# A state-space mixer's chunk stage on one core: two program blocks joined into one, with decay buffers, carried state, gate and squares placed differently

## The reference

```python
def ssd_chunked(x, dt, a, bmat, cmat):        # 256 tokens, 16 heads of 64, 2 groups, state 128
    l = SSD_CHUNK                              # 128, so c = 2 chunks
    xd = (x * dt[..., None]).reshape(b, c, l, g, r, p)
    a_cs = cumsum((dt * a) within a chunk)
    seg = exp(where(causal, a_cs[l] - a_cs[s], -inf))
    cb = einsum('bclgn,bcsgn->bcgls', cm, bm)
    y_diag = einsum('bcgrls,bcsgrp->bclgrp', cb * seg, xd)
    states = einsum('bclgn,bcgrl,bclgrp->bcgrpn', bm, exp(a_cs[-1] - a_cs), xd)
    y_off = einsum('bclgn,bcgrpn,bcgrl->bclgrp', cm, state carried in, exp(a_cs))
    return y_diag + y_off
...
    y = ssd_chunked(...) + xs * d_skip         # mamba2_branch
    y = y * silu(z)
    yg = y * rsqrt(mean(y * y over the group) + eps)
    return yg * norm_w
```

## Time and profile before

| | us |
|---|---|
| median of 3 runs | 2144.39 (2143.79 to 2147.41) |
| profiled execution | 2136.68 |
| its span, first to last instruction | 2134.7 |
| PE busy in the span | 1880.7 |
| DVE busy | 1016.3 |
| ACT busy | 589.1 |
| mean granted TensorE clock | 0.898 of full |

### The profile page before, as it was taken

How to read it: one execution, slowest core, us unless ns; L and a number is a source line. 1 busy time by engine, 2 the same in 40 slices (tenths; PEclk the granted TensorE clock), 3 DMA queues, 4 the chain that set the end, 5 groups by cost and what they waited for, 6 DMA issues and landing times. The chain is left out here.

```text
span 2134.7 us, 33193 instructions
## 1 busy us (share of the span) xinstructions
PE 1880.7 (88%) x14404; PEld 1474.7 (69%) x14404; DVE 1016.3 (48%) x1903; ACT 589.1 (28%) x865; POOL 25.5 (1%) x16
## 2 busy tenths in 40 slices
PE   4999999789999699989984799979996996758998
PEld 3544356574443599968863699979995875547997
DVE  5122243332222566623474565656666156656664
ACT  3000012320000533312241443344332222024332
POOL 0000000000000100000000010010000000001000
PEclk8789899787998899999976899999998998579999
DMA  6799960359999555414210355535550411034540
GB/s 271 327 424 425 425 255 19 134 207 359 425 424 425 218 184 191 153 60 181 98 58 0 119 181 194 178 128 183 183 183 23 167 55 61 4 138 141 194 158 20
DMA packets 57993, 404.28 MB, mean 189 GB/s; under 512 B 6352, under 2 KB 7760, under 8 KB 10224
## 3 DMA queue, kind: packets, MB, share of 16 engines
q1 hardware_dynamic: 57840, 402.07, 49.5%
HBM read 400.99 MB, written 1.05 MB: 188 GB/s over the span
## 5 line engine op out<-in xcount | busy, mean ns | idle before, releaser
L1717 PE MATMUL ps<-ffn_xh,ffn_wh 128*128 128x256 f32 x1408 | 405.2, 288 | 28.5 <-DVE ffn_xl L1832 28.5
L1718 PE MATMUL ps<-ffn_xl,ffn_wh 128*128 128x256 f32 x1408 | 403.5, 287 | 0.0
L1719 PE MATMUL ps<-ffn_xh,ffn_wl 128*128 128x256 f32 x1408 | 403.1, 286 | 0.0
L1808 DVE TENSOR_TENSOR ffn_wl<-w,ffn_wh 128x2048 fp32r<-128x2048 f32 (+1 forms) x136 | 304.3, 2237 | 15.9 <-ACT ffn_wh L1774 14.7
L1717 PEld LDWEIGHTS ps<-ffn_xh,ffn_wh 128*128 128x128 f32 x1408 | 275.7, 196 | 31.1 <-DVE ffn_wl L1808 29.5
L1718 PEld LDWEIGHTS ps<-ffn_xl,ffn_wh 128*128 128x128 f32 x1408 | 275.7, 196 | 1.6
L1719 PEld LDWEIGHTS ps<-ffn_xh,ffn_wl 128*128 128x128 f32 x1408 | 275.5, 196 | 0.0
L1774 ACT CAST ffn_wh<-w 128x2048 fp32r<-128x2048 f32 (+1 forms) x136 | 247.1, 1842 | 18.4 <-PEq L2229 8.2
L1815 DVE TENSOR_TENSOR ffn_zg<-ps,rs 128x256 f32<-128x256 f32 x88 | 37.4, 425 | 247.8 <-PE ps L1719 247.6
L1788 ACT ACTIVATE ffn_sil<-ffn_zg 128x256 f32<-128x256 f32 x88 | 36.8, 418 | 419.6 <-DVE ffn_zg L1815 419.6
L1717 PE MATMUL ps<-ffn_wh,ffn_hidh 128*128 128x512 f32 x352 | 137.4, 390 | 0.0
(11 more groups left out here) (481 smaller groups left out, 2829.2 us busy)
## 6 DMA issues: line engine op xcount, KB each, us to landing
w<-in_ffn_gu SPq DMA_DIRECT2D x88, 1024.0 KB, 5.0
w<-in_moe_gu SPq DMA_DIRECT2D x78, 1024.0 KB, 16.0
w_extra<-in_moe_gu SPq DMA_DIRECT2D x50, 1024.0 KB, 21.0
w<-in_ffn_dn SPq DMA_DIRECT2D x44, 1024.0 KB, 5.0
w_extra<-in_moe_dn SPq DMA_DIRECT2D x32, 1024.0 KB, 18.0
w<-in_moe_dn SPq DMA_DIRECT2D x32, 1024.0 KB, 21.5
w<-in_ab_xbc SPq DMA_DIRECT2D x6, 1024.0 KB, 4.8
w<-in_ab_out SPq DMA_DIRECT2D x6, 1024.0 KB, 4.9
```

The source lines that it names most:

```text
L1717: nc.tensor.matmul(out, wh, xh, start=start, stop=False)
L1718: nc.tensor.matmul(out, wh, xl, start=False, stop=False)
L1719: return nc.tensor.matmul(out, wl, xh, start=False, stop=stop)
L1808: nc.vector.tensor_tensor(low[:, s, at], S.buf(units[n])[:, at], high[:, s, at], ALU.subtract).then_inc(*w_split.one())
```

## The change

`ssd_chunks` becomes one block. The sum computed is the same; what moves:

- `seg` has three buffers (u % 3). On DVE, weigh(u) stands ahead of relative(u + 1).
- On PE, decays(0) and decays(1) stand among the transposes, and decays(u + 2) stands behind values(u). The state's two products stand behind decays(4), and what the state gives to chunk 1 behind decays(6). The B features and `cb` use banks 7 and 6 at first, the transposes of `xs` banks 2 to 5, which are also those of values.
- ACT begins with the Silu of `z`, then the two small Exps; it copies chunk 1's `xs` from banks 4 and 5 behind exp(0) and exp(1). Its squares write a buffer `junk` instead of `xd`; those of chunk 0 follow exp(7), those of chunk 1 wait for its gate, and each waits for the one before.
- On DVE, one more step stands between relative(u) and weigh(u) or between two units: `xd` of chunk 1, the skip product of either chunk, the copy of the state, and for chunk 0 adding the products and the gate. After the loop the carried part is scaled into a buffer `off` and added in one instruction for both groups, and then chunk 1 has its products added and its gate.

The diff, cut; the removed side is the function printed above:

```diff
-        seg = sb("ssd_seg", [P, 2, 4, P])
+        seg = sb("ssd_seg", [P, 3, 4, P])
...
+            def decays(u):
+                if u >= 2:
+                    pe.wait_ge(*s_ready.at(u - 1))
...
+            def values(u):
+                pe.wait_ge(*ready.at(u + 1))
+                pe.wait_ge(*xd_made.at(c + 1))
...
+            turn_x(0)
+            decays(0)
+            turn_x(1)
...
+            decays(1)
+            turn_x(2)
+            turn_x(3)
...
+            for u in range(n):
+                if u == 4:
+                    pe.wait_ge(*xs_taken.at(2))
+                values(u)
+                if u + 2 < n:
+                    decays(u + 2)
+                if u == 2:
+                    states()
+                if u == 4:
+                    carried()
...
+            nc.scalar.activation(z[:], z[:], ACT.Silu)
+            nc.scalar.activation(acs[:, 0, 1], acs[:, 0, 1], ACT.Exp)
+            nc.scalar.activation(acs[:, 1, 2], acs[:, 1, 0], ACT.Exp).then_inc(*e_done.one())
...
+            for u in range(n):
+                act.wait_ge(*s_ready.at(u + 1))
+                nc.scalar.activation(seg[:, u % 3], seg[:, u % 3], ACT.Exp).then_inc(*e_made.one())
+                if u < 2:
+                    act.wait_ge(*made.at(4 + u))
+                    nc.scalar.copy(xs[:, 1, 512 * u:512 * u + 512], K.ps[:, 4 + u]).then_inc(*xs_taken.one())
+            link(act, K.act_step, squares(0))
+            link(act, K.act_step, squares(1))
...
+            def relative(u):
+                dve.wait_ge(*s_made.at(u + 1))
+                if u >= 3:
+                    dve.wait_ge(*y_made.at(u - 2))
...
+            def gate(c):
+                dve.wait_ge(*y_made.at(4 * c + 4))
...
+            weigh(1)
+            relative(2)
+            dve.wait_ge(*xs_taken.at(2))
+            v.tensor_tensor(hp(xd[:, 1]), hp(xs[:, 1]), heads(dt[:, 1]), ALU.mult).then_inc(*xd_made.one())
+            weigh(2)
+            relative(3)
+            skip(0)
+            weigh(3)
+            relative(4)
+            dve.wait_ge(*st_made.at(1))
+            v.tensor_copy(state[:], K.ps[:, 6:8].rearrange("p g n -> p g n")).then_inc(*st_taken.one())
+            weigh(4)
+            relative(5)
...
+            skip(1)
+            weigh(5)
+            relative(6)
+            gate(0)
+            weigh(6)
+            relative(7)
+            weigh(7)
```

More of the change, by code:

```diff
@@ L2315, in ssd_chunks @@
     hp = lambda ap: ap.rearrange("p (h d) -> p h d", d=HD)
+    wide = lambda ap: ap.rearrange("p (h a) -> p h a", a=1)
+    units = [(c, g, q) for c in range(2) for g in range(SSD_GROUPS) for q in range(2)]
+    n = len(units)
     with ExitStack() as ctx:
@@ L2323, in ssd_chunks @@
         state = sb("ssd_state", [P, SSD_GROUPS, HG * HD])
+        off = sb("ssd_off", [P, SSD_INNER])
+        junk = sb("ssd_junk", [P, 512])
+        seg = sb("ssd_seg", [P, 3, 4, P])
         ms = sb("ssd_ms", [P, 2, SSD_GROUPS, 2])
[L2325 to L2336, removed]
-                mm.then_inc(*made.one())
[L2338 to L2342, removed]
@@ new lines, in ssd_chunks @@
+        made, xs_taken, e_done = K.sig("tile_made"), K.sig("fill_taken"), K.sig("exp_done")
+        st_in, st_made, st_taken, off_made = K.sig("exp_asked"), K.sig("t_made"), K.sig("t_taken"), K.sig("o_taken")
+        s_made, s_ready, e_made, ready, y_made = K.sig("s_made"), K.sig("s_ready"), K.sig("e_made"), K.sig("p_ready"), K.sig("pv_made")
+        xd_made, gated, rooted = K.sig("x_ready"), K.sig("gated"), K.sig("rooted")
+        block = ctx.enter_context(nc.Block())
+        @block.sync
@@ L2346, in _ @@
                 mm.then_inc(*st_made.one())
[L2348 to L2372, removed]
@@ L2374, in ssd_chunks, with carried @@
-        units = [(c, g, q) for c in range(2) for g in range(SSD_GROUPS) for q in range(2)]
-        n = len(units)
-        seg = sb("ssd_seg", [P, 2, 4, P])
[L2377 to L2386, removed]
+            def carried():
+                pe.wait_ge(*st_taken.at(1))
@@ L2387, in _ @@
                 for g in range(SSD_GROUPS):
                     mm = nc.tensor.matmul(K.ps[:, 6 + g], cv[:, 10 + g, P:2 * P], state[:, g], start=True, stop=True)
[L2389 to L2441, removed]
-                dve.wait_ge(*y_made.at(n))
-                dve.wait_ge(*y_off.at(1))
-                for c in range(2):
-                    do(v.tensor_tensor(hp(xs[:, c]), hp(xs[:, c]), wide(row[:, 2]).to_broadcast([P, 16, HD]), ALU.mult))
-                    for g in range(SSD_GROUPS):
-                        part = xs[:, c, g * 512:(g + 1) * 512]
-                        do(v.tensor_tensor(part, part, K.ps[:, 2 + 2 * c + g], ALU.add))
-                        if c == 1:
-                            tmp = xdd[:, g * 512:(g + 1) * 512]
-                            do(v.tensor_tensor(hp(tmp), hp(K.ps[:, 6 + g]), wide(acs[:, 1, 2, g * HG:(g + 1) * HG]).to_broadcast([P, HG, HD]), ALU.mult))
-                            do(v.tensor_tensor(part, part, tmp, ALU.add))
-                last = v.tensor_tensor(xs[:], xs[:], z[:], ALU.mult)
-                last.then_inc(*used.one())
-                dve.wait_ge(*used.at(2))
-                do(v.reciprocal(ms[:, :, :, 0:1], ms[:, :, :, 1:2]))
-                for c in range(2):
-                    for g in range(SSD_GROUPS):
-                        at = g * 512
-                        last = v.scalar_tensor_tensor(out=joined[:, c, 512 + at:1024 + at], in0=xs[:, c, at:at + 512], scalar=ms[:, c, g, 0:1],
-                                               in1=normw[:, at:at + 512], op0=ALU.mult, op1=ALU.mult)
@@ new lines, in carried @@
+                mm.then_inc(*off_made.one())
+            turn_x(0)
+            decays(0)
+            turn_x(1)
+            for c in range(2):
+                for g in range(SSD_GROUPS):
+                    t = slice(c * P, (c + 1) * P)
+                    mm = nc.tensor.matmul(K.ps[:, 6, (2 * c + g) * P:(2 * c + g + 1) * P], cv[:, 8 + g, t], cv[:, 10 + g, t], start=True, stop=True)
+            mm.then_inc(*made.one())
+            decays(1)
+            turn_x(2)
+            turn_x(3)
@@ new lines, in _ @@
+            for g in range(SSD_GROUPS):
+                mm = nc.tensor.transpose(K.ps[:, 7, g * P:(g + 1) * P], cv[:, 8 + g, 0:P], K.con(C_ID))
+            mm.then_inc(*made.one())
+            for u in range(n):
[8 more added lines that the diff above has]
+                    carried()
@@ new lines, in _, with squares @@
+        @block.scalar
+        def _(act):
+            nc.scalar.activation(z[:], z[:], ACT.Silu)
+            nc.scalar.activation(acs[:, 0, 1], acs[:, 0, 1], ACT.Exp)
+            nc.scalar.activation(acs[:, 1, 2], acs[:, 1, 0], ACT.Exp).then_inc(*e_done.one())
+            def squares(c):
+                act.wait_ge(*gated.at(c + 1))
+                for g in range(SSD_GROUPS):
+                    last = nc.scalar.activation(junk[:], xs[:, c, g * 512:(g + 1) * 512], ACT.Square, accum_out=ms[:, c, g, 0:1])
+                    if g < SSD_GROUPS - 1:
+                        link(act, K.act_step, last)
+                return last
+            for u in range(n):
[6 more added lines that the diff above has]
+            link(act, K.act_step, squares(1))
+            nc.scalar.activation(ms[:, :, :, 1:2], ms[:, :, :, 0:1], ACT.Sqrt, bias=K.eps[:, 1:2], scale=1.0 / (HG * HD)).then_inc(*rooted.one())
```

71 lines of the change are left out of this document (added).

## The result

| | before | after |
|---|---|---|
| median | 2144.09 us (2141.49 to 2147.41, 4 runs) | 2108.82 us (2107.87 to 2113.50, 4 runs) |
| traced execution | 2136.68 | 2108.55 |
| its span | 2134.7 | 2106.8 |
| the stage in it | 68.06 | 40.85 |
| ahead of the stage | 1110.50 | 1109.62 |

The recorded ratio is 0.9844 (95% interval 0.9828 to 0.986), which is 33 us of gain (30 to 37); the two medians lie 35.3 us apart. The stage of the trace did almost what was worked out: 27.2 us less for 26.9. So the question is where the other 6 to 8 us are: the two traces differ by 27.9 us in span, the medians by 35.3.

What follows compares the result with a forecast made beforehand. The prediction took engines waiting for each other as the bound. Start 3.87, DVE's work 30.87 and tail 6.40 us replaced the 68.06 us stage: 26.9 us less, 2144.39 to 2117.5 us, range 2112 to 2125.

Steps and rivals of the forecast that it cites:

- What bounds the stage, and where its waits are: Changed stage: engines wait for each other; DVE waited 19.5 us for PE's decays, ACT 26.3 us for DVE's relative.
- Part 1: Loop: DVE's 2.82 us covers PE's 2.14, so DVE stops waiting except 0.79 us at weigh(7); third buffer costs nothing.
- Part 2: Stage start: DVE's second copy of chunk 0's `xs` starts 3.87 us after PE; remaining PE and ACT work costs nothing.
- Part 3: DVE's work from the second copy to the end of chunk 1's gate sums to 30.87 us.
- Part 4: Tail from the gate's end to PE's next start: two squares instead of four, 6.40 us instead of 7.49.
- The step that failed: From traced execution to median: 26.9 us, found in the trace, taken off the median 2144.39 too, giving 2117.5.
- The range: Around the forecast time: 2112 to 2125 us as the range of 8 in 10, including 3 us for scatter of medians.
- Rival A: Clock falls in the changed loop and PE becomes the bound: gain 15.9 us, 2128.5, or 2123 if halfway; 18%.
- B: Loop keeps 3.90 us a unit and only the moved ends gain: 22.9 us, 2121.5; 8%.
- C: Stage shortens but the next work waits for something else, no measurable gain: 2144; 3%.
- D: Clock stays low beyond the stage, so the output projection behind it runs slower: plus 5.7 us, 2150; 3%.

Runs made afterwards that it cites:

- a_two: The changed kernel with two decay buffers instead of three, and the wait on a buffer's release one unit earlier: 2106.2 us, stage 40.86 us.
- b_copy3: The kernel before, unchanged, run again for a further trace: traced execution 2144.3 us, stage 74.57 us.
- b_copy4: The kernel before, unchanged, run again for a further trace: traced execution 2144.4 us, stage 76.73 us.
- b_ring: The kernel before with only DVE's loop order changed, weigh(u) ahead of relative(u + 1): 2128.3 us, ratio 0.9934, stage 56.94 us.
- b_busy: The kernel before with one more product on PE behind each group of decays from unit 1 on: 2134.96 us, ratio 0.9975, stage 64.01 us.
- b_copy: The kernel before, unchanged, run again for a second trace: median 2138.6 us, traced execution 2143.76 us, stage 74.61 us.
- b_copy2: The kernel before, unchanged, run again for a further trace: traced execution 2146.9 us, stage 76.73 us.
- b_busy2: The kernel before with the same added PE product as b_busy, run again for a second trace: 2135.22 us, ratio 0.996, stage 63.75 us.
- a_best: The changed kernel shortened at both ends (earlier decays and steps, early table load, chunk 1's gate split by group): 2106.4 us, ratio to before 0.9839, stage 36.57 us.

## Why the prediction was wrong

- **What bounds the stage, and where its waits are:** right. The ring of decays, relative, Exp, weigh and values was the bound at both readings of the clock, 1.00 and 0.50.
- **Part 1:** right. DVE never waits for PE inside the loop, relative(2) to relative(6) stand 2.81 to 2.93 us apart for 2.82, the Exp wait is 0.7 for 0.79. That the third buffer costs and brings nothing is shown by `a_two`.
- **Part 2:** the second copy began 3.69 us after PE's first transpose (1109.62 to 1113.31), for 3.87.
- **Part 3:** the DVE chain from there to the end of the last gate is 30.70 us (1113.31 to 1144.01) for 30.87.
- **Part 4:** 6.46 us for 6.40. The stage in all is 40.85 for 41.14.
- **The step that failed** is the one between the trace and the median: "The median of the runs, 2144.39, is 7.7 us above it; I take the same difference off it." With it the sum took 68.06 us, the stage of one execution, for the stage of the median. The 7.7 us were not a constant beside the stage: two later executions at the median's time, `b_copy3` and `b_copy4`, have 6.5 and 8.7 us more in the stage and 1.2 more and 1.0 less outside it. In the traced execution four of the six steps between relative(1) and relative(7) took 3.90 us and two 5.63; in the other four traces of that code at least five take 5.63, and the stage is 74.6 to 76.7 us. The clock of the changed loop reads 1.00 up to values(7) in all three of its traces, with stages of 40.85, 40.85 and 40.86 us. So the gain is 74.1 - 40.9 = 33.2 us by the mean of the traces. Taken together over the chips, all executions of before (71, the first traced one among them) have a median of 2141.4 us and those of the changed kernel with either number of buffers (14) 2108.8: 32.6 us. The first comparison has an interval of 30 to 37 us (1.4 to 1.72% of 2144), which leaves 26.9 out and holds 33.
- **The range** was too narrow as well. Its 3 us for "how far medians of this kernel lie apart (2143.79 to 2147.41)" came from three single executions; the 71 lie between 2127.6 and 2148.9.
- **Rival A** was looked for on the wrong side. I asked whether the clock would fall in the changed loop, and priced half clock there; I had the rows of before at half clock (5.63 us a unit) in hand and did not ask what before would take if all its units were so. That is 68.06 + 4 x 1.73 = 75.0 us (the four steps at 3.90), close to the four other traces, and a forecast from it would have been 2144.4 - 33.9 = 2110.5. My words that the clock "stayed through five units with 2.05 us of work in 3.90" took one execution for the rule (and what shows there are four steps of 3.90). That 2110.5 lies near the measured 2108.8 is worked out afterwards, with the copies known.
- **The gaps of PE:** they did not tell the two loops apart. PE was 21.89 us busy of 31.5 with the clock at 0.50 in one trace of before, and 11.71 of 20.4 at 1.00 in another of the same code. The changed kernel's PE also has gaps, ahead of five of the eight groups of values (0.21 to 1.50 us), and its clock reads 0.99. So the prediction was right not to expect the fall in the changed loop, but it did not ask what the fall at 1143.5 in its own trace meant for before.
- **Rivals B, C and D** did not occur; `b_ring` shows that the order on DVE alone takes the ring from 3.90 us to 2.46.

Still open: why the timed executions of `b_busy` are 6 us and not 10 below before.

## What to carry over

This ring, in which TensorE waited 1.85 us a unit, lost twice: the wait itself, and the clock, which read 0.50 from values(0) or decays(2) on in four traces of the same code and from 1143.5, ahead of values(4), in the other (5.63 us a unit instead of 3.90). If the profile shows part of a loop at half clock and part at full, take the loop at both as bounds for the time before as well as after, and look whether the traced execution's time is that of the median; here the trace 7.7 us faster than the median was the untypical one of five.
To shorten such a ring, first ask whether an engine does the next item's first step ahead of this item's last one: swapping these two gave 17 us of the stage here (11 us by the medians), one more buffer gave nothing, and work moved into the loop only the waits it covers.

## What the runs showed of the hardware

- The same code, in the same loop, takes 3.90 us a unit with the clock at 1.00 and 5.63 at 0.50 (`before`, `b_copy`). With 2.05 us of PE work in 3.90 the clock stayed at 1.00 for four steps in one trace (`before`); in the four others it fell in the first one, during values(0) (1.77 us in `b_copy`, 1.76 in `b_copy3`, for 1.10) or decays(2) (2.02 us in `b_copy2`, 2.01 in `b_copy4`, for 1.11), and read 0.50 in the rest of the loop. With one more product a unit, which adds 0.86 us of work, it read 1.00 through the loop in both traces (`b_busy`, `b_busy2`).
- In `a_best` a root of a constant, 0.20 us, loads the table early: the 1.28 us of the load then lie beside DVE's work, and the Squares and the root behind it needed no other load.
- Two DVE instructions of 512 columns, each recorded as 0.68 to 0.69 us, start 0.72 to 0.73 us apart when the second waits for the first, and 0.60 to 0.61 apart when it doesn't (`after`, `before`); with 1024 columns (1.22 to 1.23) it is 1.25 to 1.26 and 1.14.
